# A ring of nine gathered rows, with weight loads of one 512 KB tile instead of two at a time

## The chip, the cores and the metric

The kernel runs on one core of one Trainium2 chip. The metric is device time in microseconds (us) of one execution, lower is better. Before the change three runs gave a median of 2445.37 us (2445.34 to 2450.84).

## The reference, cut to what matters

A block of 512 tokens by 1024 channels, all in fp32. Per token, after two mixers, come a product with an output matrix, a product with a query matrix, and the PEER layer: the queries are scored against two sets of 128 keys, the 16 best pairs for each of 8 heads name 128 experts out of 16384, and for each of them the layer computes

```python
dot = h @ u[expert]                # u and v rows of 1024 numbers
y  += gate * gelu(dot) * v[expert]
```

The kernel keeps u and v side by side (`peer_uv`), so one expert is one row of 8 KB. Then a second block follows: an input product of six 512-column tiles (`w_in_2`), two kinds of attention, an output product (`w_out_2`), and a gated feed-forward layer with 2816 hidden channels (`w_gu`, `w_down_2`).

## The kernel before, in words

Tokens are worked on in four blocks of 128. The program has a front part (to about 329 us), then `stage_first` (to about 1982 us), which runs the PEER layer for all four blocks and beside it the second block's work for the first 256 tokens, and `stage_half`, the second block's work for the last 256 tokens, alone.

**Gather** (class `Gather`). A slot is one (block, expert place): 512 slots. For slot n GpSimd issues an indirect DMA (L1123) that fetches one row of 8 KB for each of the 128 tokens, 1 MB in all, into buffer n mod RING of `uv_ring`. RING is the eighth argument at L2539, 8 before. VectorE takes the dot product with the u half (L1275), ScalarE the gelu, the weight (L1325) and a diagonal matrix of the weights (L1334), and TensorE multiplies it with the v half in four passes (L1355). In the last block each fourth slot is added by VectorE instead (L1229). Gather n waits until slot n - RING has been added (`added`).

**Weights** (class `Weights`, L1391 to L1450). All other products of these two stages take their weights as tiles of 256 by 512 numbers, 512 KB. A tile goes through three steps: SyncE loads it into a raw buffer (`loads`, L1413), ScalarE rounds it to a high part (`highs`, L1427), VectorE or GpSimd subtracts that from the raw tile for the low part (`lows`, L1435), and TensorE makes twelve matmuls of it (`product`, L1446 to L1448). Before the change a load carries a pair of tiles, 1 MB, and there are two raw buffers of a pair. Load m, of tiles 2m and 2m+1, waits until the low part of tile 2m-3 is done:

```python
if m >= self.RAW:
    sp.wait_ge(self.s_lo, 2 * (m - self.RAW + 1))
```

There are `SPLIT` buffers for high and low parts, two in `stage_first` and three in `stage_half`; `highs` waits until TensorE has used tile n - SPLIT. `stage_first` takes 146 tiles: `Tail` a (24, partly before the gather), `Tail` b (24), `In2` (24), `Out2` (8), `Ffn` (66). `stage_half` takes 98.

**Order of work.** Each engine's program is one list, merged by `weave` from several streams by planned places in us. The plan gives a slot 2.6 us and a tile 2.8 us (`Tail` a), 9.0 us (`Tail` b) or 4.2 us (`In2`, `Out2`, `Ffn` of the first half). Each engine then runs its list in order, so what waits holds back all that stands behind it on that engine. Loads are placed 20 us ahead of their tile; gather n is placed at the slot time of n - RING + 2.5.

Of the kernel before, what the change touches and what calls it, by code (L numbers as in the profile page):

```python
# [19 lines left out]
P = 128  # L20
S = 512
D = 1024
KD = D // P
TB = S // P
# [37 lines left out]
class Chain:  # L62
# [3 lines left out]
    def __init__(self, eng, sem):  # L66
        self.eng, self.sem, self.n, self.base = eng, sem, 0, 0
# [103 lines left out]
class Columns:  # L171
# [11 lines left out]
    def loads(self, sp):  # L183
        for n in range(len(self.src)):
            self.load(sp, n)
# [830 lines left out]
class Gather:  # L1016
# [189 lines left out]
    def dve(self, dve):  # L1206
# [55 lines left out]
        for place, _, b, s in queue:  # L1262
# [33 lines left out]
        for q in range(self.n - G, self.n):  # L1296
            if self.here(q):
                add(q)
# [87 lines left out]
class Weights:  # L1386
# [4 lines left out]
    def __init__(self, K, ctx, raw, split, us):  # L1391
        self.K, self.us, self.src, self.at = K, us, [], []
        self.RAW, self.SPLIT, self.LEAD = raw, split, split - 1
        self.raw = [K.sb(ctx, f"w_raw{r}", [P, 2 * self.KK, 512]) for r in range(self.RAW)]
        self.hi = [K.sb(ctx, f"w_high{r}", [P, self.KK, 512], F32R) for r in range(self.SPLIT)]
        self.lo = [K.sb(ctx, f"w_low{r}", [P, self.KK, 512], F32R) for r in range(self.SPLIT)]
        self.s_land = [K.sem(f"weights_landed{r}") for r in range(self.RAW)]
        self.s_hi, self.s_lo, self.s_used = K.sem("weights_high"), K.sem("weights_low"), K.sem("weights_used")

    def add(self, pairs, places):  # L1400

        first = len(self.at)
        assert len(places) == 2 * len(pairs)
        self.src += pairs
        self.at += places
        return first

    def loads(self, sp):
        for m, src in enumerate(self.src):
            yield self.at[2 * m] - 20.0  # L1410
            if m >= self.RAW:
                sp.wait_ge(self.s_lo, 2 * (m - self.RAW + 1))
            sp.dma_start(self.raw[m % self.RAW][:, :, :], src).then_inc(self.s_land[m % self.RAW], 16)  # L1413

    def tile(self, n):
        return self.raw[n // 2 % self.RAW][:, self.KK * (n % 2):self.KK * (n % 2 + 1), :]

    def place(self, n):
        return max(self.at[n - self.LEAD], self.at[n] - 15.0) if n >= self.LEAD else self.at[0] - 5.0

    def highs(self, act):
        for n in range(len(self.at)):
            yield self.place(n)
            act.wait_ge(self.s_land[n // 2 % self.RAW], 16 * (n // 2 // self.RAW + 1))
            if n >= self.SPLIT:
                act.wait_ge(self.s_used, n - self.SPLIT + 1)
            act.copy(self.hi[n % self.SPLIT][:, :, :], self.tile(n)).then_inc(self.s_hi, 1)  # L1427

    def lows(self, eng, first=0, last=None):
        for n in range(first, len(self.at) if last is None else last):  # L1430
            yield self.place(n)
            if n == first and n:
                eng.wait_ge(self.s_lo, n)
            eng.wait_ge(self.s_hi, n + 1)
            eng.tensor_tensor(self.lo[n % self.SPLIT][:, :, :], self.tile(n),  # L1435
                               self.hi[n % self.SPLIT][:, :, :].bitcast(F32), ALU.subtract).then_inc(self.s_lo, 1)

    def product(self, pe, n, rows, banks, k0, first, last):
# [143 lines left out]
class In2:  # L1582
# [4 lines left out]
    def __init__(self, K, W, plan, half, h, nat, one=False):  # L1587
        self.K, self.W, self.h, self.half, self.nat, self.one = K, W, h, half, nat, one
        self.nb = half.nb
        self.CH = KD // W.KK  # L1590
        self.at = plan.take([W.us] * (6 * self.CH) + [half.tail_us])
        self.first = W.add([K.i["w_in_2"][self.TILE[t], c] for t in self.ORDER for c in range(self.CH // 2)],
                           self.at[:6 * self.CH])
# [464 lines left out]
class Out2:  # L2058


    def __init__(self, K, W, plan, half, mix, banks):
        self.K, self.W, self.half, self.mix, self.banks, self.nb = K, W, half, mix, banks, half.nb
        self.CH = KD // W.KK
        self.at = plan.take([W.us] * (2 * self.CH))
        self.first = W.add([K.i["w_out_2"][n, c] for n in range(2) for c in range(self.CH // 2)], self.at[:2 * self.CH])
        self.s_x = K.sem("out2_added")

    def pe(self, pe):
# [18 lines left out]
class Ffn:  # L2087
# [4 lines left out]
    def __init__(self, K, W, plan, half, h, up, acc):  # L2092
        self.K, self.W, self.half, self.h, self.up, self.acc, self.nb = K, W, half, h, up, acc, half.nb
        self.CH = KD // W.KK
        lengths, tiles, self.order = [], [], []
        for g in range(self.G + 1):
            if g < self.G:
                for c in range(self.CH):
                    self.order.append(("up", g, c))
                tiles += [K.i["w_gu"][g, c] for c in range(self.CH // 2)]  # L2100
            if g:
                self.order.append(("down", g - 1, 0))
                tiles.append(K.i["w_down_2"][g - 1])
            if g < self.G:
                self.order.append(("turn", g, 0))
            if g:
                self.order.append(("down", g - 1, 1))
        self.lag = half.lag
# [112 lines left out]
class Tail:  # L2221
# [4 lines left out]
    def __init__(self, K, W, plan, b0, x, split, keep, us, gap, before=None, prompt=0):  # L2226
# [5 lines left out]
        self.first_o = W.add([K.i["w_out_1"][n, c] for n in range(2) for c in range(self.CH // 2)], self.at_o[:2 * self.CH])  # L2232
# [7 lines left out]
        self.first = W.add([K.i["w_peer_q"][j, c] for j in range(self.G) for c in range(self.CH // 2)],  # L2240
                           self.at_p[:self.G * self.CH])
        self.end = self.at_p[-1]
        self.at_t = [self.rowed(j) + 1.0 if j < prompt else self.at_p[self.CH * (j + 1) + 2] for j in range(self.G - 1)]
# [290 lines left out]
def stage_first(K, half, x):  # L2534

    nc, nb = K.nc, half.nb
    with ExitStack() as c1:
        half.place(c1, x[0:nb], False)
        g = Gather(K, c1, list(range(TB)), x, 0.0, 2.6, (6, 7), 8, 4, 3)  # L2539
        W, plan, un = Weights(K, c1, 2, 2, half.tile_us), Plan(), half.mix  # L2540
        begin = g.at(nb * SLOTS + 4)
        four = [K.ps[j][:, :] for j in range(4)]
# [129 lines left out]
def stage_half(K, half, x):  # L2672

    nc, nb = K.nc, half.nb
    with ExitStack() as ctx:
        half.place(ctx, x, True)
        half.place_queries(ctx)
        W, plan = Weights(K, ctx, 2, 3, half.tile_us), Plan()
        un = half.spare.rearrange("p (b d) -> p b d", b=nb)
        four = [K.ps[j][:, :] for j in range(4)]  # L2680
        at = plan.take([half.tail_us])
# [127 lines left out]
def _pairs(_np, w):  # L2809

    r, c = w.shape
    return w.reshape(r // 512, 4, 128, c // 512, 512).transpose(3, 0, 2, 1, 4)


def _columns(_np, w):

    return w.reshape(KD, P, -1, P).transpose(2, 1, 0, 3).reshape(-1, P, D)
# [37 lines left out]
```

## Time and profile before

| | |
|---|---|
| median of three runs | 2445.37 us |
| the profiled execution's own time | 2446.69 us |
| its span (first to last instruction) | 2445.0 us |
| TensorE busy | 2046.7 us (84%) |
| VectorE busy | 1501.4 us (61%) |
| ScalarE busy | 995.8 us (41%) |
| GpSimd busy | 920.9 us (38%) |
| bytes moved by DMA | 726.58 MB, 540.59 of them on the gather's queue |
| 1 MB weight loads in all | 122: 73 in the first stage, 49 in the second |

Busy shares are means over stages with different limits. The DMA line of the page, in 40 slices of 61 us, shows which stages keep the 16 DMA engines full. A `_a` at the end of a name is `stage_first`, `_b` is `stage_half`. GB/s divided by the share of the DMA engines in a window tells at what rate they work while they are busy.

### The profile page before, as it was taken

How to read it: one execution, taken by the hardware profiler on the slowest of the kernel's cores; microseconds unless marked ns; L12 is line 12 of the kernel's file. 1: busy time of each engine (PE TensorE's matmuls, PEld its weight loads, DVE VectorE, ACT ScalarE, POOL GpSimd, SP SyncE). 2: the span in 40 equal slices, each digit the busy share in tenths (PEclk: the TensorE clock that was granted, in tenths of full speed). 3: DMA queues.
4: the chain of work that ended last, by engine and by line, in shares of the span. 5: the costliest groups of instructions: out<-in, count | busy, mean ns of one | idle time of the engine just before them, and what ended most of it. 6: DMA issues, size and time to landing. Idle time of an engine off the chain costs nothing. (4 is left out here: it accounts for less than half of the span.)

```text
span 2445.0 us, 22099 instructions
## 1 busy us (share of the span) xinstructions
PE 2046.7 (84%) x7187; PEld 1273.7 (52%) x7187; DVE 1501.4 (61%) x2987; ACT 995.8 (41%) x2304; POOL 920.9 (38%) x681
## 2 busy tenths in 40 slices
PE   7997867897898777777899888879999968687999
PEld 4776645553554222222465334446666547456787
DVE  4748546788895677755678876667777732442111
ACT  3205443434233222232545577444344334344443
POOL 3522002333444433333223444233343326005887
PEclk8986678999999999999899999889999989798999
DMA  7720035999999999999899999999999934002554
GB/s 266 271 93 1 1 137 204 378 421 378 421 394 391 418 421 422 421 421 421 340 384 388 417 372 369 376 369 383 421 421 421 421 142 145 18 1 99 177 190 155
DMA packets 111071, 726.58 MB, mean 297 GB/s; under 512 B 12520, under 2 KB 13547, under 8 KB 29803
## 3 DMA queue, kind: packets, MB, share of 16 engines
q0 software_dynamic: 74800, 540.59, 54.2%
q1 hardware_dynamic: 35520, 184.43, 20.2%
q8 instruction: 57, 0.93, 0.2%
q14 instruction: 60, 0.48, 0.1%
q10 hardware_dynamic: 634, 0.14, 0.0%
HBM read 716.45 MB, written 8.66 MB: 297 GB/s over the span
## 5 line engine op out<-in xcount | busy, mean ns | idle before, releaser
L1355 PE MATMUL ps<-uv_ring_a,expert_diag_a 128*128 128x512 f32 x1920 | 906.8, 617 | 213.8 <-ACT expert_diag_a L1334 195.0
L1123 POOL DMA_INDIRECT uv_ring_a<-in_peer_uv_dram,expert_idx x512 | 582.2, 1137 | 958.1 <-PE ps L1355 918.3
L1275 DVE CUSTOM_DVE_ANT_0 uv_ring_a<-uv_ring_a,x_rows 128x1024 f32<-128x1024 f32 x512 | 620.4, 1219 | 170.8 <-DMA uv_ring_a<-in_peer_uv_dram,expert_idx 170.0
L1355 PEld LDWEIGHTS ps<-uv_ring_a,expert_diag_a 128*128 128x128 f32 x1920 | 364.0, 196 | 674.6 <-issue 362.2
L1319 ACT ACTIVATE expert_gelu_a<-expert_dot_a 128x2 f32<-128x2 f32 x256 | 52.1, 204 | 782.9 <-DVE expert_dot_a L1275 782.7
L1435 POOL TENSOR_TENSOR w_low_b<-w_raw_b,w_high_b 128x1024 fp32r<-128x1024 f32 x98 | 233.7, 2395 | 256.5 <-ACT w_high_b L1427 255.5
L1435 DVE TENSOR_TENSOR w_low_a<-w_raw_a,w_high_a 128x1024 fp32r<-128x1024 f32 x142 | 173.6, 1223 | 192.2 <-ACT w_high_a L1427 191.5
L1427 ACT CAST w_high_a<-w_raw_a 128x1024 fp32r<-128x1024 f32 x146 | 151.0, 1038 | 97.3 <-PE ps L1448 85.4
L1334 ACT ACTIVATE expert_diag_a<-ident,expert_weight_a 128x128 f32<-128x128 f32 x480 | 168.6, 395 | 0.6 <-ACT expert_weight_a L1325 0.6
L1427 ACT CAST w_high_b<-w_raw_b 128x1024 fp32r<-128x1024 f32 x98 | 102.7, 1052 | 122.3 <-PE ps L1448 68.2
L1325 ACT ACTIVATE expert_weight_a<-expert_gelu_a,expert_gate 128x1 f32<-128x1 f32 x512 | 122.8, 286 | 8.9
L1446 PE MATMUL ps<-w_high_a,turned_high_a 128*128 128x512 f32 x208 | 101.3, 487 | 5.8 <-DVE ffn_low_a L2200 5.7
L1446 PE MATMUL ps<-w_high_a,tail_turned_high_a 128*128 128x512 f32 x192 | 89.0, 463 | 17.6 <-DVE w_low_a L1435 11.7
L2190 DVE SCALAR_TENSOR_TENSOR ffn_silu_b<-ffn_silu_b,ps 128x256 f32<-128x256 f32 x22 | 9.2, 417 | 142.2 <-ACT ffn_silu_b L2172 142.2
L1446 PE MATMUL ps<-w_high_b,turned_high_b 128*128 128x512 f32 x208 | 82.6, 397 | 3.9 <-DVE turned_low_b L1484 3.9
L1448 PE MATMUL ps<-w_high_a,turned_low_a 128*128 128x512 f32 x208 | 83.4, 401 | 0.0
L1447 PE MATMUL ps<-w_low_a,turned_high_a 128*128 128x512 f32 x208 | 83.0, 399 | 0.0
L1447 PE MATMUL ps<-w_low_b,turned_high_b 128*128 128x512 f32 x208 | 82.3, 396 | 0.0
L1448 PE MATMUL ps<-w_high_b,turned_low_b 128*128 128x512 f32 x208 | 82.1, 395 | 0.0
L1447 PE MATMUL ps<-w_low_a,tail_turned_high_a 128*128 128x512 f32 x192 | 77.7, 405 | 0.0
L1448 PE MATMUL ps<-w_high_a,tail_turned_low_a 128*128 128x512 f32 x192 | 77.4, 403 | 0.0
L203 POOL TENSOR_TENSOR in_low<-in_raw,in_high 128x1024 fp32r<-128x1024 f32 x20 | 54.4, 2725 | 55.3 <-ACT in_high L198 55.2
(460 smaller groups left out, 3279.1 us busy)
## 6 DMA issues: line engine op xcount, KB each, us to landing
w_raw_a<-in_w_gu_dram SPq DMA_DIRECT2D x22, 1024.0 KB, 9.0
w_raw_b<-in_w_gu_dram SPq DMA_DIRECT2D x22, 1024.0 KB, 4.9
w_raw_a<-in_w_peer_q_dram SPq DMA_DIRECT2D x16, 1024.0 KB, 9.2
w_raw_a<-in_w_out_dram SPq DMA_DIRECT2D x12, 1024.0 KB, 9.0
w_raw_a<-in_w_in_dram SPq DMA_DIRECT2D x12, 1024.0 KB, 9.8
w_raw_b<-in_w_in_dram SPq DMA_DIRECT2D x12, 1024.0 KB, 4.9
w_raw_a<-in_w_down_dram SPq DMA_DIRECT2D x11, 1024.0 KB, 9.1
w_raw_b<-in_w_down_dram SPq DMA_DIRECT2D x11, 1024.0 KB, 4.9
```

Of the source, the lines that this page charges most:

```text
L203: pool.tensor_tensor(self.lo[n % self.SPLIT][:, :], self.raw[n % self.RAW][:, :], self.hi[n % self.SPLIT][:, :].bitcast(F32), ALU.subtract ...
L1123: pool.indirect_dma_start(out=self.ring[:, n % self.RING, :], out_offset=None, in_=K.uv, in_offset=bass.IndirectOffsetOnAxis(ap=K.idx[self ...
L1275: dve.tensor_tensor_reduce(u, u, self.h[b][:, :], 1.0, 0.0, ALU.mult, ALU.add, self.a[:, s:s + 1]).then_inc(self.s_dot, 1)
L1319: act.activation(self.gl[:, c], self.a[:, c], ACT.Gelu).then_inc(self.s_gelu, 1)
L1325: act.activation(self.w[:, i:i + 1], self.gl[:, i:i + 1], ACT.Copy, scale=K.gate[self.blocks[b] % 2][:, i:i + 1]).then_inc(self.s_w, 1)
L1334: act.activation(self.diag[q % self.DIAGS][:, :], K.ident[:, :], ACT.Copy, scale=self.w[:, i:i + 1]).then_inc(self.s_diag, 1)
L1355: ins = nc.tensor.matmul(self.bank(half), self.diag[q % self.DIAGS][:, :], self.ring[:, n % self.RING, D + 512 * half:D + 512 * half + 512 ...
L1427: act.copy(self.hi[n % self.SPLIT][:, :, :], self.tile(n)).then_inc(self.s_hi, 1)
L1435: eng.tensor_tensor(self.lo[n % self.SPLIT][:, :, :], self.tile(n), self.hi[n % self.SPLIT][:, :, :].bitcast(F32), ALU.subtract).then_inc( ...
L1446: nc.tensor.matmul(bank, rh, hi[:, kk, :], start=first and kk == 0, stop=False)
L1447: nc.tensor.matmul(bank, rh, lo[:, kk, :], start=False, stop=False)
L1448: ins = nc.tensor.matmul(bank, rl, hi[:, kk, :], start=False, stop=last and kk == self.KK - 1)
```

## The change

The ring gets a ninth buffer (8 KB per partition). The raw weight buffers hold one tile in place of two: in `stage_first` two of 512 KB in place of two of 1 MB, in `stage_half` four of 512 KB in place of two of 1 MB. Each load carries one tile; load n waits for the low part of tile n - 2 (first stage) or n - 4 (second). The weights are laid out in DRAM tile by tile, so a partition's piece of a load is 4 KB in place of 8 KB. No instruction of ScalarE, VectorE, GpSimd or TensorE is added or removed; SyncE issues 244 weight loads in place of 122.

```diff
-        self.raw = [K.sb(ctx, f"w_raw{r}", [P, 2 * self.KK, 512]) for r in range(self.RAW)]
+        self.raw = [K.sb(ctx, f"w_raw{r}", [P, self.KK, 512]) for r in range(self.RAW)]
...
     def loads(self, sp):
-        for m, src in enumerate(self.src):
-            yield self.at[2 * m] - 20.0
-            if m >= self.RAW:
-                sp.wait_ge(self.s_lo, 2 * (m - self.RAW + 1))
-            sp.dma_start(self.raw[m % self.RAW][:, :, :], src).then_inc(self.s_land[m % self.RAW], 16)
+        for n, src in enumerate(self.src):
+            yield self.at[n] - 20.0
+            if n >= self.RAW:
+                sp.wait_ge(self.s_lo, n - self.RAW + 1)
+            sp.dma_start(self.raw[n % self.RAW][:, :, :], src).then_inc(self.s_land[n % self.RAW], 16)
...
     def highs(self, act):
-        for n in range(len(self.at)):
+        for n in range(len(self.src)):
             yield self.place(n)
-            act.wait_ge(self.s_land[n // 2 % self.RAW], 16 * (n // 2 // self.RAW + 1))
+            act.wait_ge(self.s_land[n % self.RAW], 16 * (n // self.RAW + 1))
...
-        g = Gather(K, c1, list(range(TB)), x, 0.0, 2.6, (6, 7), 8, 4, 3)
+        g = Gather(K, c1, list(range(TB)), x, 0.0, 2.6, (6, 7), 9, 4, 3)
         W, plan, un = Weights(K, c1, 2, 2, half.tile_us), Plan(), half.mix
...
-        W, plan = Weights(K, ctx, 2, 3, half.tile_us), Plan()
+        W, plan = Weights(K, ctx, 4, 3, half.tile_us), Plan()
...
-    inputs["w_peer_q"] = _pairs(_np, inputs["w_peer_q"][0])
-    for name in ("w_in_2", "w_out_2"):
-        inputs[name] = _pairs(_np, inputs[name][0])
+    inputs["w_peer_q"] = _tiles(_np, inputs["w_peer_q"][0])
+    for name in ("w_in_2", "w_out_2", "w_down_2"):
+        inputs[name] = _tiles(_np, inputs[name][0])
```

The other edits of the diff let `Tail`, `In2`, `Out2` and `Ffn` name single tiles in place of pairs to `Weights.add`. `_pairs` laid out four rows of 128 by 512 per load, `_tiles` lays out two.

## Rows read from the trace of the kernel before

**Rows 1.** The page: the DMA engines' busy tenths in 40 slices.
```profile
DMA  7720035999999999999899999999999934002554
```

**Rows 2.** Windows: us, busy per engine (instructions), clock, DMA share, GB/s.
```profile
750.00:1150.00 400.00, 293.93 (x668) 119.73 (x667) 252.96 (x582) 106.88 (x397) 159.17 (x156) 0.98 1.01 417
...
1550.00:1700.00 150.00, 129.22 (x415) 79.68 (x416) 100.90 (x150) 66.83 (x152) 49.86 (x43) 0.92 0.90 366
1700.00:1950.00 250.00, 238.84 (x827) 153.82 (x826) 188.28 (x272) 99.00 (x255) 96.84 (x78) 0.99 1.01 421
```

**Rows 3.** Waits in 413 to 1968 us: total us, times, longest.
```profile
POOL uv_ring_a L1123 <- PE ps L1355: 918.3, 418, 16.3
...
DVE uv_ring_a L1275 <- DMA uv_ring_a<-in_peer_uv_dram,expert_idx: 170.0, 162, 3.3
```

**Rows 4.** Windows of the large dips of the DMA share, columns as in rows 2.
```profile
440.00:451.00 11.00, 11.00 (x50) 7.95 (x49) 8.85 (x23) 4.70 (x14) 3.04 (x3) 1.00 0.71 264
586.00:594.00 8.00, 8.00 (x13) 3.48 (x14) 6.32 (x25) 6.33 (x15) 2.71 (x2) 0.68 0.43 148
...
1170.00:1178.00 8.00, 6.72 (x22) 3.69 (x23) 3.78 (x16) 2.12 (x8) 1.87 (x2) 0.70 0.43 150
1181.00:1188.00 7.00, 6.84 (x15) 3.53 (x16) 6.61 (x17) 2.69 (x8) 2.62 (x2) 0.76 0.44 146
...
1549.00:1558.00 9.00, 6.36 (x9) 2.77 (x10) 8.51 (x13) 1.93 (x5) 0.94 (x1) 0.62 0.37 127
...
1618.00:1626.00 8.00, 7.25 (x18) 4.05 (x19) 5.97 (x9) 2.91 (x9) 2.37 (x2) 0.79 0.41 146
1652.00:1658.00 6.00, 6.00 (x19) 3.60 (x18) 3.43 (x4) 2.33 (x2) 2.11 (x2) 0.95 0.47 160
```

**Rows 5.** GpSimd's timeline at the dip of 586 to 594 us.
```profile
590.04 1.77 POOL L1123 DMA_INDIRECT uv_ring_a<-in_peer_uv_dram,expert_idx  x1 [9.20 <-PE ps L1355]
```

**Rows 6.** DMA in 1700 to 1900 us: queue, packets, MB, share; a load's median us.
```profile
q1 hardware_dynamic: 2769, 20.19, 24.3%
...
w_raw_a<-in_w_gu_dram SPq DMA_DIRECT2D x13, 1024.0 KB, 9.0
```

**Rows 7.** DMA in 926 to 937 us, then a load in 1535 to 1546.
```profile
q1 hardware_dynamic: 144, 0.52, 11.8%
...
route_scores_a<-s_dram SPq DMA_DIRECT2D x1, 512.0 KB, 8.0
...
x_rows<-x_rows_dram SPq DMA_DIRECT2D x1, 512.0 KB, 8.4
```

**Rows 8.** DMA in 1960 to 1970 us, after the last gather; then in 2250 to 2440.
```profile
x_rows<-x_rows_dram SPq DMA_DIRECT2D x1, 512.0 KB, 3.5
...
w_raw_b<-in_w_gu_dram SPq DMA_DIRECT2D x19, 1024.0 KB, 4.9
```

**Rows 9.** Timelines of VectorE and ScalarE before the gather starts.
```profile
343.90 1.23 DVE L1435 TENSOR_TENSOR w_low_a<-w_raw_a,w_high_a 128x1024 fp32r<-128x1024 f32 x1 [5.07 <-ACT w_high_a L1427]
...
348.32 1.05 ACT L1427 CAST w_high_a<-w_raw_a 128x1024 fp32r<-128x1024 f32 x1 [1.71 <-PE ps L1448]
```

**Rows 10.** The same two timelines just after the gather has started.
```profile
413.28 1.22 DVE L1435 TENSOR_TENSOR w_low_a<-w_raw_a,w_high_a 128x1024 fp32r<-128x1024 f32 x1
...
417.74 1.05 ACT L1427 CAST w_high_a<-w_raw_a 128x1024 fp32r<-128x1024 f32 x1 [1.42 <-PE ps L1448]
```

**Rows 11.** The tile's instructions in 1700 to 1950 us, and one tile's steps there.
```profile
L1435 DVE TENSOR_TENSOR w_low_a<-w_raw_a,w_high_a x48: 1210/1225/1227, 1699.6 to 1947.9; 128x1024 fp32r<-128x1024 f32 x48
...
1753.77 1.23 DVE L1435 TENSOR_TENSOR w_low_a<-w_raw_a,w_high_a 128x1024 fp32r<-128x1024 f32 x1 [2.33 <-ACT w_high_a L1427]
...
1760.78 1.05 ACT L1427 CAST w_high_a<-w_raw_a 128x1024 fp32r<-128x1024 f32 x1 [1.50 <-PE ps L1448]
...
1762.80 1.22 DVE L1435 TENSOR_TENSOR w_low_a<-w_raw_a,w_high_a 128x1024 fp32r<-128x1024 f32 x1
```

**Rows 12.** TensorE's timeline at the start of the second stage.
```profile
1999.79 0.76 PE L1446 MATMUL ps<-w_high_b,in_turned_high_b 128*128 128x512 f32 x1 [8.21 <-POOL w_low_b L1435]
```

More of the change, by code:

```diff
@@ L1398, in __init__, with add @@
         self.s_hi, self.s_lo, self.s_used = K.sem("weights_high"), K.sem("weights_low"), K.sem("weights_used")
[L1400 to L1404, printed above, removed]
+    def add(self, tiles, places):
+        first = len(self.src)
+        self.src += tiles
         self.at += places
@@ L1408, in loads @@
     def loads(self, sp):
-        for m, src in enumerate(self.src):
-            yield self.at[2 * m] - 20.0
-            if m >= self.RAW:
-                sp.wait_ge(self.s_lo, 2 * (m - self.RAW + 1))
-            sp.dma_start(self.raw[m % self.RAW][:, :, :], src).then_inc(self.s_land[m % self.RAW], 16)
-    def tile(self, n):
-        return self.raw[n // 2 % self.RAW][:, self.KK * (n % 2):self.KK * (n % 2 + 1), :]
+        for n, src in enumerate(self.src):
[3 more added lines that the diff above has]
+            sp.dma_start(self.raw[n % self.RAW][:, :, :], src).then_inc(self.s_land[n % self.RAW], 16)
     def place(self, n):
@@ L1421, in highs @@
     def highs(self, act):
-        for n in range(len(self.at)):
+        for n in range(len(self.src)):
             yield self.place(n)
-            act.wait_ge(self.s_land[n // 2 % self.RAW], 16 * (n // 2 // self.RAW + 1))
+            act.wait_ge(self.s_land[n % self.RAW], 16 * (n // self.RAW + 1))
             if n >= self.SPLIT:
                 act.wait_ge(self.s_used, n - self.SPLIT + 1)
-            act.copy(self.hi[n % self.SPLIT][:, :, :], self.tile(n)).then_inc(self.s_hi, 1)
+            act.copy(self.hi[n % self.SPLIT][:, :, :], self.raw[n % self.RAW][:, :, :]).then_inc(self.s_hi, 1)
     def lows(self, eng, first=0, last=None):
-        for n in range(first, len(self.at) if last is None else last):
+        for n in range(first, len(self.src) if last is None else last):
             yield self.place(n)
@@ L1434, in lows @@
             eng.wait_ge(self.s_hi, n + 1)
-            eng.tensor_tensor(self.lo[n % self.SPLIT][:, :, :], self.tile(n),
+            eng.tensor_tensor(self.lo[n % self.SPLIT][:, :, :], self.raw[n % self.RAW][:, :, :],
                                self.hi[n % self.SPLIT][:, :, :].bitcast(F32), ALU.subtract).then_inc(self.s_lo, 1)
@@ L1591, in __init__ @@
         self.at = plan.take([W.us] * (6 * self.CH) + [half.tail_us])
-        self.first = W.add([K.i["w_in_2"][self.TILE[t], c] for t in self.ORDER for c in range(self.CH // 2)],
+        self.first = W.add([K.i["w_in_2"][self.TILE[t], c] for t in self.ORDER for c in range(self.CH)],
                            self.at[:6 * self.CH])
@@ L2064, in __init__ @@
         self.at = plan.take([W.us] * (2 * self.CH))
-        self.first = W.add([K.i["w_out_2"][n, c] for n in range(2) for c in range(self.CH // 2)], self.at[:2 * self.CH])
+        self.first = W.add([K.i["w_out_2"][n, c] for n in range(2) for c in range(self.CH)], self.at[:2 * self.CH])
         self.s_x = K.sem("out2_added")
@@ L2099, in __init__ @@
                     self.order.append(("up", g, c))
-                tiles += [K.i["w_gu"][g, c] for c in range(self.CH // 2)]
+                    tiles.append(K.i["w_gu"][g, c])
             if g:
                 self.order.append(("down", g - 1, 0))
-                tiles.append(K.i["w_down_2"][g - 1])
+                tiles.append(K.i["w_down_2"][0, g - 1])
             if g < self.G:
@@ L2107, in __init__ @@
                 self.order.append(("down", g - 1, 1))
+                tiles.append(K.i["w_down_2"][1, g - 1])
         self.lag = half.lag
@@ L2231, in __init__ @@
         self.at_o = plan.take([us] * (2 * self.CH))
-        self.first_o = W.add([K.i["w_out_1"][n, c] for n in range(2) for c in range(self.CH // 2)], self.at_o[:2 * self.CH])
+        self.first_o = W.add([K.i["w_out_1"][n, c] for n in range(2) for c in range(self.CH)], self.at_o[:2 * self.CH])
         self.at_n = plan.take([gap, gap])
@@ L2239, in __init__ @@
         self.at_p += plan.take([us / 2] * 4)
-        self.first = W.add([K.i["w_peer_q"][j, c] for j in range(self.G) for c in range(self.CH // 2)],
+        self.first = W.add([K.i["w_peer_q"][j, c] for j in range(self.G) for c in range(self.CH)],
                            self.at_p[:self.G * self.CH])
@@ L2806, in _tiles @@
     return w.reshape(r // 256, 2, 128, c // 512, 512).transpose(3, 0, 2, 1, 4)
-def _pairs(_np, w):
-    r, c = w.shape
-    return w.reshape(r // 512, 4, 128, c // 512, 512).transpose(3, 0, 2, 1, 4)
 def _columns(_np, w):
@@ L2829 @@
     gate, up = inputs.pop("w_gate_2")[0], inputs.pop("w_up_2")[0]
-    inputs["w_gu"] = _pairs(_np, _np.concatenate([gate.reshape(D, -1, 256), up.reshape(D, -1, 256)], axis=2).reshape(D, -1))
+    inputs["w_gu"] = _tiles(_np, _np.concatenate([gate.reshape(D, -1, 256), up.reshape(D, -1, 256)], axis=2).reshape(D, -1))
     inputs["c_columns"] = inputs.pop("c")[0].reshape(KD, P).T
@@ L2841 @@
     wo = inputs.pop("w_out")[0]
-    inputs["w_out_1"] = _pairs(_np, _np.concatenate([wo[0:512], wo[512:][heads]]))
-    inputs["w_peer_q"] = _pairs(_np, inputs["w_peer_q"][0])
-    for name in ("w_in_2", "w_out_2"):
-        inputs[name] = _pairs(_np, inputs[name][0])
-    inputs["w_down_2"] = inputs["w_down_2"][0].reshape(-1, 2, 128, 2, 512).transpose(0, 2, 3, 1, 4).reshape(-1, 128, 4, 512)
+    inputs["w_out_1"] = _tiles(_np, _np.concatenate([wo[0:512], wo[512:][heads]]))
+    inputs["w_peer_q"] = _tiles(_np, inputs["w_peer_q"][0])
+    for name in ("w_in_2", "w_out_2", "w_down_2"):
+        inputs[name] = _tiles(_np, inputs[name][0])
     for name in _INS:
```

## The prediction

> **What bounds the kernel now.** I read the DMA line of the page first [rows 1]: nine tenths from slice 8 to slice 32, some 1500 of 2445 us. That is the gather. The windows say how full it is [rows 2]: from 750 to 1150 us and from 1700 to 1950 us the share is 1.01, at 417 and 421 GB/s, so nothing is left there; from 1550 to 1700 us it is 0.90. A gather moves 1.05 MB, at 421 GB/s 2.5 us. In the stretch 1700 to 1950 TensorE is also busy 238.84 of 250 us: two bounds lie within 5% of each other, and in that stretch the feed-forward tiles of the first half run between the slots.
>
> The waits say the same from the other side [rows 3]. GpSimd waits 918.3 us in 418 waits for TensorE to free a ring buffer, and VectorE 170.0 us for gathered rows. A ring that is always full is no loss while the DMA engines are full. It is one where they run dry. So I looked for the dips of the share. The large ones are short windows of their own [rows 4]. Idle time is length times (1 - share): 3.2 us at 440 to 451; then 4.6, 4.6, 3.9, 5.7, 4.7 and 3.2 us, 26.6 us in the six from 586 on. In the first of these GpSimd stood still 9.20 us until TensorE released a buffer [rows 5]: TensorE, held up by something else, freed no buffer, and the eight rows on their way ran out.
>
> **The ring of nine.** Gather n is released by slot n - 9. In each dip one more gather, 2.5 us of DMA work, is under way before the engines run dry, and as the stretch behind it is again full, the 2.5 us stay won. Every one of the six dips is longer than that. The four up to 1558 us give 4 x 2.5 = 10 us. The two behind lie where TensorE is nearly full too, and I count half, 2.5 us. So -12.5 us. Ends: 0 (TensorE's hold-up grows by what the ring adds), and -26.6 us, all that was idle there.
>
> The dip at 440 is dealt with below. The ring adds no instruction; GpSimd issues the same 512 gathers, each placed 2.6 us earlier, and the only other work on its list in that stage, four low parts and the loads before the gather, is planned ahead of the first gather either way.
>
> **Single tiles: what a load takes.** Beside the gather a 1 MB load lands 9.0 us after issue [rows 6]. For 512 KB with 4 KB per partition there are loads of just this shape, of scores and of token rows: 8.0 and 8.4 us [rows 7]. Half the bytes save one microsecond, no more, since each packet still stands in line behind a gathered row's. Without the gather it is 3.5 us against 4.9 us for 1 MB [rows 8]. I take 8.0 and 3.5.
>
> A weight load may start when the low part of tile n - 2 is done; before, of tile 2m - 3, so three to four tiles ahead. The loop of one buffer is load, high, low: with the gather 8.0 + 0.05 to issue + 1.05 + 1.22 + 0.1 for two handovers = 10.4 us, for two tiles.
>
> **Before the gather.** Tile 4's high part starts at 348.32, 3.2 us after the low part of tile 2 ended (343.90 + 1.23) [rows 9]. The load needs 3.5. So 0.3 us is lost where tiles follow closely. There are two such runs before the gather, of six and eight tiles, and the loss shows in every second tile at most: 1 us of the path, since the routing that starts the gather waits for these products. Ends 0 and 4 (a 512 KB load beside other loads, 4.9 in place of 3.5, in three places).
>
> **The gather's start.** Now the first eight gathers fill the DMA queues while the last six tiles of `Tail` a are still to come. The high part at 417.74 stands 3.2 us after the low part that ended at 414.50 [rows 10]; the load takes 8.0, so it is 4.8 us late, and its successors lose a little more. TensorE does the first slots between these tiles, so the ring opens late, and the dip at 440 to 451 grows by about that; the ninth buffer gives 2.5 us back. I take +4. Ends 0 and 8.
>
> **`Tail` b, `In2`, `Out2`.** `Tail` b is planned at 9.0 us a tile, 18 for two, against a loop of 10.4: hidden. `In2` and `Out2` are 32 tiles in which DMA or TensorE sets a pace somewhat above that of the feed-forward part, and I count nothing; if that cover is gone, they are part of the second rival. On SyncE a load that waits holds back stores and loads of rows and scores behind it. Each has its loads spaced a tile apart now, so the wait of one is shorter, and I count nothing.
>
> **The feed-forward tiles of the first half.** 48 low parts from 1699.6 to 1947.9 [rows 11] are (1947.9 - 1699.6) / 47 = 5.28 us a tile, 10.57 us for two. The loop is 10.4. It fits with 0.17 us to spare, if nothing comes between. Something does: the tile shown [rows 11] had its high part at 1760.78, done at 1761.83, and its low part at 1762.80, 0.97 us later, since VectorE was at something else. By its load it would be later still: 1755.00 + 0.05 + 8.0 = 1763.05, 2.3 us behind 1760.78. Most tiles are done some microseconds before TensorE wants them, and that lead takes up single delays, but not a loop that is too long in the mean. I take half of the 0.97 as the mean delay in a loop: 10.4 + 0.49 - 10.57 = 0.3 us for two tiles, 33 times, 10 us, and of these 8 kept, as TensorE's idle 4.5% takes up some. Behind a late load ScalarE holds the diagonals too, which is in the same 8. Ends 0 and 27: with a load of 9.0, as the 1 MB one has, the loop is 11.4, which is 0.83 too long for two tiles, 33 times.
>
> **Twice the packets.** A half MB cost 11.8% of 11 us, 1.30 us, as 4 KB pieces [rows 7], and 24.3% of 200 us for 20.19 MB, 1.26 us, as 8 KB pieces [rows 6]. 0.04 us for each of 128 tiles beside the gather is 5 us if the DMA engines were the bound throughout; I take 3, ends 0 and 5. SyncE's 122 additional issues are hidden, it is idle nearly always.
>
> The Trainium skill ("DMA: Bandwidth & Descriptors", Rules for kernel authors) asks for 1 MiB or more per DMA for the best bandwidth, which speaks against this change. Its fit there, 2.0 us plus bytes / 436e3, gives an estimate of 3.2 us for 512 KB and 4.4 for 1 MB; without the gather the rows agree nearly (3.5, 4.9), with it they don't (8.0, 9.0), and by that fit the 8 us of the feed-forward part and the 4 at the gather's start would be none, and the sum 12 us lower.
>
> **The second stage.** TensorE waits 8.21 us for the first tile's low part, until 1999.79 [rows 12]. The first load is 1 MB, and half of it would land 0.5 MB / 421 = 1.2 us sooner: -1.2 us. With four tiles in flight and 3.5 us a load the later loads are early by several microseconds instead of just in time, but TensorE hardly waits for them now. Ends 0 and -3.
>
> **Sum.** -12.5 + 1 + 4 + 8 + 3 - 1.2 = +2.3 us on the profiled execution's 2446.7 us, so 2449.0. That execution is 1.3 us above the median of the runs, and against the median I say 2448. What this kernel's measurement can tell from no change is about 0.3%, 7.3 us: the forecast is no change (chance 0.38).
>
> **Rivals.**
> *Weights become the bound (slower, 0.37).* Place: feed-forward tiles between slots, 1600 to 1970 us, and the 24 tiles of `In2`. It decides as soon as the loop of load, high and low takes over 10.6 us. For it: 10.4 from rows without any delay in it. Against it: when TensorE stalls, fewer gathers are released and a load then waits less. Price at 9.0 us per load or a like delay: 27 + 8 at the start + 1 + 3, less the ring's 10 before that stretch and 1.2: +28, which is 2474.
> *The ring's gain comes whole and the loads stay hidden (faster, 0.25).* -26.6 + 1 + 4 + 3 - 1.2 = -20: 2426. With 15 (2.5 in each of six dips) it would be -8: 2437. For it: the dips are there, and each began with a full ring. Against it: TensorE's hold-ups aren't shortened by a ring, only bridged.
> *The ring does nothing* since the DMA engines are full, and the loads cost what I say: +15, 2461, inside the slower case.
> *The change doesn't do what it says:* the raw buffers and the ring have the same bytes before and after, and gather n has a buffer of its own, so I give that nothing.
>
> The range that leaves out no more than 2 in 10 is 2431 to 2477; the forecast's own is 2440 to 2453. Faster by over 0.3%: 0.25. Within: 0.38. Slower: 0.37.
>
> **What would show it.** In the profile after: a 512 KB weight load at 8.0 to 8.4 us beside the gather and about 3.5 in the second stage; the dips at about 590, 1170, 1185 and 1550 us shorter by 2.5 us each; waits of ScalarE at L1427 for the landing of raw tiles, of which there are hardly any in the gather now, and waits of TensorE for low parts; more than 5.3 us a tile after 1700 us; TensorE's first tile of the second stage 1.2 us sooner behind its transposes. Wrong would be: loads of 6 us or less beside the gather (then the faster case), or dips that are as long as before (then the ring gave nothing), or 1.01 of share in the feed-forward part with a span as before though loads are late.

## The result, and the profile after

The kernel after the change takes 2472.35 us (median of 4 runs, 2467.99 to 2475.6), against 2445.36 before. The ratio is 1.0107, with a 95% interval of 1.0084 to 1.0131: 26 us slower, and the range of that is 21 to 32. The forecast was 2448, no change; the time is within 2 us of the first rival's (2474). The profiled execution has a span of 2473.2 us, 28.2 above before.

The page's DMA line, to be laid beside [rows 1]. It hardly tells that anything was lost: only slices 8 and 27 fell from nine to eight, and in the feed-forward stretch, slices 28 to 32, all are still nines. (A slice is 61.8 us now, 61.1 before.)

```profile
DMA  7720045899999999999899999989999945003664
```

Two windows as in [rows 2]. In 250 us of the feed-forward stretch TensorE now does 768 matmuls in place of 827, VectorE 250 instructions in place of 272, and the DMA engines move 395 GB/s in place of 421. That is 6% less, while their busy share went from 1.01 to 0.99, 2% less: the share alone would not have told it. TensorE, VectorE and ScalarE all do less in the same time, and none of the three is full: something that they all wait for sets the pace. It isn't TensorE's clock, granted at 0.97 in place of 0.99 here: over the first stage the same 208 product matmuls took 487 ns each before and 488 after (L1446 and L1441 on the pages).

```profile
1550.00:1700.00 150.00, 120.33 (x381) 74.02 (x382) 96.56 (x146) 63.82 (x148) 47.54 (x40) 0.91 0.91 363
1700.00:1950.00 250.00, 227.40 (x768) 143.79 (x767) 173.97 (x250) 92.79 (x235) 90.33 (x73) 0.97 0.99 395
```

The loads, from the page's list of DMA issues (KB each, median us to landing). Half the bytes take 7.9 us beside the gather, where 1 MB took 9.0 [rows 6], and 3.6 us in the second stage, where it took 4.9 [rows 8].

```profile
w_raw_a<-in_w_gu_dram SPq DMA_DIRECT2D x44, 512.0 KB, 7.9
w_raw_b<-in_w_gu_dram SPq DMA_DIRECT2D x44, 512.0 KB, 3.6
```

Then the waits in 413 to 2000 us (engine, line, waited for: total us, times, longest). ScalarE stands and waits for a weight load in 37 places, 106 us in all. Before, the same list had one such row, 4.0 us, shown last. A wait isn't yet a cost: the longest, 13.7 us at a `w_out` tile at 489 us, stands as 12.8 us in the kernel r8_four too, which is level with before.

```profile
ACT w_high_a L1422 <- DMA w_raw_a<-in_w_down_dram: 28.7, 13, 4.6
ACT w_high_a L1422 <- DMA w_raw_a<-in_w_gu_dram: 23.3, 9, 4.0
ACT w_high_a L1422 <- DMA w_raw_a<-in_w_peer_q_dram: 23.3, 7, 5.6
ACT w_high_a L1422 <- DMA w_raw_a<-in_w_out_dram: 17.1, 3, 13.7
PE ps L1441 <- DVE w_low_a L1430: 13.7, 7, 3.2
ACT w_high_a L1422 <- DMA w_raw_a<-in_w_in_dram: 13.6, 5, 6.3
...
ACT w_high_a L1427 <- DMA w_raw_a<-in_w_out_dram: 4.0, 1, 4.0
```

The pace of the tiles, to set beside [rows 11], and the landing times of that stretch (min, median, max): (1945.4 - 1700.8) / 43 = 5.69 us a tile in place of 5.28. The four lines between say how long an engine stood idle before the instructions of this stretch, and how often: VectorE until ScalarE's cast was done, 42 times in 44 subtractions; ScalarE until the load landed, 11 and 7 times in 45 casts, or until TensorE was done with a buffer, 2 times.

```profile
L1430 DVE TENSOR_TENSOR w_low_a<-w_raw_a,w_high_a x44: 1219/1225/1228, 1700.8 to 1945.4; 128x1024 fp32r<-128x1024 f32 x44
...
  ACT w_high_a L1422: 76.0, 42
  DMA w_raw_a<-in_w_down_dram: 25.3, 11
  DMA w_raw_a<-in_w_gu_dram: 15.9, 7
  PE ps L1443: 4.8, 2
...
DMA to landing us min/median/max: 4.3/7.8/9.6
```

At the gather's start ScalarE's timeline shows the six last tiles of `Tail` a, each of them now released by its load. The last cast is at 446.52, 35.1 us after the first gather (411.4). Before, it was at 437.38 (last line), 24.2 us after the first gather (413.2).

```profile
420.11 1.04 ACT L1422 CAST w_high_a<-w_raw_a 128x1024 fp32r<-128x1024 f32 x1 [5.20 <-DMA w_raw_a<-in_w_peer_q_dram]
...
446.52 1.05 ACT L1422 CAST w_high_a<-w_raw_a 128x1024 fp32r<-128x1024 f32 x1 [3.61 <-DMA w_raw_a<-in_w_peer_q_dram]
...
437.38 1.05 ACT L1427 CAST w_high_a<-w_raw_a 128x1024 fp32r<-128x1024 f32 x1 [1.43 <-PE ps L1448]
```

Before the gather little is lost. SyncE's timelines begin the stage with its first weight loads, after and then before: 85.9 us (411.4 - 325.5) and 84.1 us (413.2 - 329.1) ahead of the first gather.

```profile
325.49 24.72 SPq L1411 DMA_DIRECT2D w_raw_a<-in_w_out_dram  x7
...
329.10 19.13 SPq L1413 DMA_DIRECT2D w_raw_a<-in_w_out_dram  x4
```

The dips of [rows 4], found again in the trace of after. Idle time is 4.6, 2.6, 3.8, 1.4, 4.5 and 4.3 us, in place of 4.6, 4.6, 3.9, 5.7, 4.7 and 3.2: 21.2 in place of 26.6. Two are shorter, the one at 1174 us by 2.0 and the one at the change to the last block by 4.3; the other four are about as long as before, or longer.

```profile
594.00:604.00 10.00, 8.73 (x15) 3.87 (x16) 8.05 (x28) 7.61 (x19) 3.44 (x3) 0.70 0.54 197
1174.00:1181.00 7.00, 6.71 (x24) 3.68 (x24) 2.98 (x12) 1.60 (x6) 1.87 (x2) 0.80 0.63 222
1184.00:1192.00 8.00, 8.00 (x22) 4.39 (x21) 6.92 (x21) 3.38 (x11) 2.53 (x2) 0.81 0.53 190
1558.00:1563.00 5.00, 5.00 (x13) 2.35 (x12) 4.79 (x7) 2.50 (x9) 2.71 (x2) 0.89 0.72 259
1623.00:1632.00 9.00, 8.21 (x21) 4.66 (x22) 6.67 (x10) 2.95 (x9) 3.21 (x2) 0.81 0.50 178
1655.00:1664.00 9.00, 9.00 (x27) 5.92 (x26) 4.09 (x6) 3.92 (x5) 2.81 (x2) 0.83 0.52 181
```

And TensorE's first tile of the second stage waits 7.06 us for its low part, in place of 8.21 [rows 12].

```profile
2028.75 0.76 PE L1441 MATMUL ps<-w_high_b,in_turned_high_b 128*128 128x512 f32 x1 [7.06 <-POOL w_low_b L1430]
```

Where the 28 us of the profiled execution went is told by three points in time: the first gather, the end of the third of the four blocks of 128 tokens (L1247, where VectorE adds a block's sum), and the last gather. The first gather is at 411.4 us after and at 413.2 before. From there the third block ends 1140.9 and 1135.4 us later, and the last gather is issued 1559.8 and 1531.6 us later. So the kernel after is 5 us behind when the last block begins, and loses 23 us in the last block, where the feed-forward tiles run between the slots. The lines are after and then before.

```profile
1552.35 0.69 DVE L1247 TENSOR_TENSOR expert_sum_a<-ps,gate_rows 128x512 f32<-128x512 f32 x1 [0.59 <-DMA x_rows<-x_rows_dram]
L1123 POOL DMA_INDIRECT uv_ring_a<-in_peer_uv_dram,expert_idx x512: 932/940/2222, 411.4 to 1971.2; - x171
...
1548.59 0.68 DVE L1247 TENSOR_TENSOR expert_sum_a<-ps,gate_rows 128x512 f32<-128x512 f32 x1
L1123 POOL DMA_INDIRECT uv_ring_a<-in_peer_uv_dram,expert_idx x512: 932/940/1997, 413.2 to 1944.8; - x171
```

### The profile page after: what moved, and what is told of

The parts are those of the page before. It is cut to its first block and busy times, and to the rows that moved or that the text cites. A ratio compares the mean times of both kernels' runs of the same rounds, so it can differ in the third digit from the quotient of the medians.

```text
span 2473.2 us, 22221 instructions
## 1 busy us (share of the span) xinstructions
PE 2059.6 (83%) x7187; PEld 1276.6 (52%) x7187; DVE 1499.3 (61%) x2987; ACT 996.9 (40%) x2304; POOL 926.2 (37%) x681
## 5 line engine op out<-in xcount | busy, mean ns | idle before, releaser
L1355 PE MATMUL ps<-uv_ring_a,expert_diag_a 128*128 128x512 f32 x1920 | 921.1, 626 | 217.7 <-ACT expert_diag_a L1334 198.3
L1355 PEld LDWEIGHTS ps<-uv_ring_a,expert_diag_a 128*128 128x128 f32 x1920 | 370.0, 199 | 687.4 <-issue 373.0
L1441 PE MATMUL ps<-w_high_a,tail_turned_high_a 128*128 128x512 f32 x192 | 88.8, 463 | 23.6 <-DVE w_low_a L1430 18.8
L1441 PE MATMUL ps<-w_high_a,turned_high_a 128*128 128x512 f32 x208 | 101.4, 488 | 7.6 <-DVE ffn_low_a L2196 7.5
L1441 PE MATMUL ps<-w_high_b,turned_high_b 128*128 128x512 f32 x208 | 82.6, 397 | 3.9 <-DVE turned_low_b L1479 3.9
```

The source lines that it names most:

```text
L1355: ins = nc.tensor.matmul(self.bank(half), self.diag[q % self.DIAGS][:, :], self.ring[:, n % self.RING, D + 512 * half:D + 512 * half + 512 ...
L1441: nc.tensor.matmul(bank, rh, hi[:, kk, :], start=first and kk == 0, stop=False)
```

## The experiments

Times are given as ratios to the kernel before, measured beside each kernel on the same chip, with a 95% interval. From chip to chip the median of before moved from 2443 to 2447 us, so the ratios are what is to be compared. Where two ratios are subtracted below, the difference is uncertain by 6 to 12 us. A stretch of one trace seems steadier than a whole time (r8_four and r9_both, each traced twice, took 1532.9 and 1532.1 us, and 1525.8 and 1527.3 us, from the first gather to the last), but it is one execution.

### More buffers, and the ring back to eight

**r8_two** is the kernel after with the ring of before:

```diff
-        g = Gather(K, c1, list(range(TB)), x, 0.0, 2.6, (6, 7), 9, 4, 3)
+        g = Gather(K, c1, list(range(TB)), x, 0.0, 2.6, (6, 7), 8, 4, 3)
```

> The kernel after the change with the ring put back to eight; the raw buffers stay two single tiles. Theory A (the loop of load, high part and low part over two single buffers sets the pace of the feed-forward tiles, and the ninth ring buffer wins back a part): the feed-forward part loses at least as much as after the change, a tile takes 5.6 us or more from 1700 us on, and the ring's part is missing on top: 2474 to 2490 us. Theory B (the ninth buffer does the harm: more gathered rows stand in line ahead of a weight load): the load lands sooner and the time falls back to 2445 to 2455. Theory C (smaller packets cost DMA time): within 3 us of the kernel after, 2469 to 2476.

Measured: 2484.54 us, 1.0159 (1.0121 to 1.0197). Theory A; B falls. Without the ninth buffer the single tiles cost 39 us, with it 26.

**r8_three** and **r8_four** have the ring of eight and three or four single raw buffers in the first stage (the diff is that of three; the other has a 4 there):

```diff
-        W, plan, un = Weights(K, c1, 2, 2, half.tile_us), Plan(), half.mix
+        W, plan, un = Weights(K, c1, 3, 2, half.tile_us), Plan(), half.mix
```

> Ring of eight, three single raw buffers in the first stage in place of two. Theory A: the loop of 10.4 us now covers three tiles (15.8 us), no tile is late, and ScalarE hardly waits for raw tiles after 450 us: 2443 to 2450 us, with 5.3 us a tile from 1700 us on. Theory B: the same, so it doesn't speak on B. Theory C (packets of 4 KB cost DMA time by themselves): still 10 us or more above before, 2455 to 2475.

> Ring of eight, four single raw buffers in the first stage: the bytes of before, only in four single tiles in place of two pairs. Theory A: as with three, 2443 to 2449 us, since three already hide the loop. Theory C: 2455 to 2475, as packets and loads are as small as after the change. If four are clearly faster than three (over 5 us), a loop of three buffers was still late somewhere, most likely where the gather starts.

Measured: three 2445.1 us, 1.0011 (0.9987 to 1.0035); four 2441.2 us, 0.9991 (0.9968 to 1.0014), and when measured again 0.9983 (0.9965 to 1.0001). One more buffer of 512 KB brings back 36 us of the 39 (1.0159 - 1.0011), and the kernel is then level with before within its interval. Four are not clearly faster than three; 2441.2 lies 2 us below the range expected for it. The tiles of r8_three in 1700 to 1950 us:

```profile
L1430 DVE TENSOR_TENSOR w_low_a<-w_raw_a,w_high_a x48: 1214/1224/1227, 1699.2 to 1947.8; 128x1024 fp32r<-128x1024 f32 x48
```

(1947.8 - 1699.2) / 47 = 5.29 us a tile, that of before. ScalarE waits for a raw tile five times after the first gather and never after 476 us. All loads of r8_four are as small and as many as after the change, and it is level with before: Theory C falls. What the smaller pieces cost in DMA rate shows in the windows: in 1700 to 1950 us r8_three, r8_four, r9_late4 and r9_both all move 418 GB/s, where before moves 421.

### The packets alone

**pairs_4k** is the kernel before, one load for two tiles, with the two tiles laid out apart in DRAM:

```diff
-            sp.dma_start(self.raw[m % self.RAW][:, :, :], src).then_inc(self.s_land[m % self.RAW], 16)
+            sp.dma_start(self.raw[m % self.RAW][:, :, :].rearrange("p (t k) c -> p t k c", t=2),
+                         src.rearrange("t p k c -> p t k c")).then_inc(self.s_land[m % self.RAW], 16)
```

> The kernel before (ring of eight, two pairs of 1 MB, one load for a pair), with the weights laid out as after the change, so that a partition's part of a load is two pieces of 4 KB in place of one of 8 KB. Theory A with my reading of why half a load takes nearly as long (each weight packet stands in line behind one gathered row's packet): a 1 MB load takes 11 to 13 us beside the gather in place of 9.0; the pair's loop has room for that in the feed-forward part (about 15 us between release and need), so 2445 to 2455 us. If a load's time goes by its bytes and not by its packets: 9 us as before and 2445. Theory C: 2455 or more.

Measured: 2455.14 us, 1.0040 (1.0020 to 1.0060), 10 us slower, where r8_four with the same packets isn't. That is the border between what Theory A and Theory C had been given (2455), so this run alone doesn't decide between them; r8_four does. Its trace tells no landing times for these loads beside the gather, so the 11 to 13 us expected for one stay untested; in the second stage a pair lands in 5.0 us, where it was 4.9. What the trace shows are waits of ScalarE for raw tiles, nine in all and 26.4 us, where before had one of 4.0 us (columns as above; a ninth is 1.2 us). The 8.3 us are at the gather's start, at 424 us.

```profile
ACT w_high_a L1428 <- DMA w_raw_a<-in_w_down_dram: 10.9, 6, 3.5
ACT w_high_a L1428 <- DMA w_raw_a<-in_w_peer_q_dram: 8.3, 1, 8.3
ACT w_high_a L1428 <- DMA w_raw_a<-in_w_out_dram: 6.0, 1, 6.0
...
L1123 POOL DMA_INDIRECT uv_ring_a<-in_peer_uv_dram,expert_idx x512: 932/938/2121, 407.1 to 1947.2; - x171
```

So a pair in 4 KB pieces lands later than one in 8 KB pieces, late enough to be waited for. That fits the reading that a packet stands in line behind a gathered row's packet whatever its own size; it isn't shown by a landing time. From the first gather to the last it takes 1540.1 us, where before takes 1531.6: 8.5 of the 10 us lie in that stretch.

### What a ring buffer is worth

**before_r7** is the kernel before with a ring of seven (the argument 8 at L2539 made 7).

> The kernel before with a ring of seven, loads of pairs as they are: what one ring buffer is worth while no weight is late. Theory D (each dip of the DMA share is bridged 2.5 us per buffer, in six large dips and some small ones): 12 to 25 us slower than before, 2455 to 2468. Theory E (a buffer only helps where late weights hold TensorE up, as in the pair of kernels with two single buffers): within 4 us of before, 2439 to 2447.

Measured: 2469.92 us, 1.0100 (1.0073 to 1.0127), 24 us slower, at the upper end of what Theory D gave. Theory E is out: a buffer is worth something where no weight is late. The first and the last gather issue in its trace (the kernel's start differs by several microseconds from run to run, so the difference of the two is to be read; the line of before stands above the experiments):

```profile
L1123 POOL DMA_INDIRECT uv_ring_a<-in_peer_uv_dram,expert_idx x512: 932/938/2010, 402.0 to 1961.5; - x171
```

1559.5 us against 1531.6. The DMA engines' share over the gather, windows of before and then before_r7:

```profile
413.00:1960.00 1547.00, 1307.06 (x3885) 707.33 (x3885) 1121.06 (x2333) 633.03 (x1689) 582.20 (x512) 0.96 0.98 399
```

```profile
402.00:1973.00 1571.00, 1320.21 (x3886) 710.49 (x3886) 1123.77 (x2332) 632.93 (x1689) 580.71 (x512) 0.96 0.97 393
```

### Buffers lent by memory that is free at the time

A third raw buffer beside a ring of nine would take 4 KB per partition more than the kernels before and after have; no run tried whether it fits. But two places of 8 KB per partition are idle just where tiles are late: the ninth ring buffer until gather 8, and the two route-score buffers once the last experts are chosen. **r9_late4** is the kernel after with four buffers from tile 80 on, **r9_early4** with four for tiles 0 to 23, **r9_both** has both. Tiles 0 to 23 lie in part before the gather, and gather 8 has to wait for the loan to end. `spans` says which buffers a range of tiles goes round; loads and casts look their buffer up there.

```diff
+            W.spans = [(0, 24, [0, 1, 2, 3]), (24, 48, [0, 1]), (48, 80, [0, 1]), (80, 1 << 30, [0, 1])]
+            W.raw += [g.ring[:, g.RING - 1, D * i:D * i + D].rearrange("p (k c) -> p k c", k=2) for i in range(2)]
+            W.s_land += [K.sem(f"weights_landed_in_ring{i}") for i in range(2)]
+            g.first_free = (W.s_lo, 24)
...
+        W.raw += [g.sw[i][:, :, :].rearrange("p a b -> p (a b)").rearrange("p (k c) -> p k c", k=2) for i in range(2)]
+        W.s_land += [K.sem(f"weights_landed_in_scores{i}") for i in range(2)]
+        W.spans[-1] = (80, 1 << 30, [0, 1, late, late + 1])
+        W.before[82] = [(g.s_idx, len(g.groups))]
```

> The kernel after the change (ring of nine, two single raw buffers), but from tile 80 on, the feed-forward part of the first half, two more single buffers: the tiles lie in the two route-score buffers, free once the last experts are chosen. Theory A: the 25 us that slots and tiles lose against before between tiles 82 and 145 go, the rest stays: 2443 to 2451 us, 5.3 us a tile from 1700 us on. If something else in the feed-forward part made it slow (more packets, the ring ahead of the loads), under 10 us come back: 2460 to 2472.

> The kernel after the change with four single raw buffers for the first 24 tiles alone (before and at the start of the gather): the two more lie in the ninth ring buffer, which gather 8 then takes over when the low part of tile 23 is done. Theory A: the tiles at the gather's start are no longer late, 4 to 8 us come back: 2463 to 2470 us. If the stretch behind, which is full of DMA, had made good for it anyway: within 3 us of the kernel after, 2469 to 2475.

> Both of it: ring of nine, four single raw buffers for tiles 0 to 23 and from tile 80 on, two between. Theory A with D (a ring buffer is worth 10 us or more by itself): 2430 to 2441 us, below both kernels. Theory A with E (worth nothing while no weight is late): 2440 to 2447, level with before. Over 2450: theory A is wrong on where the loss comes from.

Measured, the three beside before on one chip, the kernel after by itself (its row is that of the result):

| | us | ratio to before | interval |
|---|---|---|---|
| after | 2472.35 | 1.0107 | 1.0084 to 1.0131 |
| r9_late4 | 2450.44 | 1.0011 | 0.9991 to 1.0030 |
| r9_early4 | 2462.12 | 1.0056 | 1.0035 to 1.0077 |
| r9_both | 2437.41 | 0.9955 | 0.9936 to 0.9975 |

Four buffers for the feed-forward tiles give back 0.0096, 24 us; four at the start 0.0051, 12 us (4 to 8 had been expected); both 0.0152, 37 us, about the sum of the two. The first two are uncertain by 8 us each. The windows of the feed-forward stretch, r9_late4, are those of before again but for the GB/s (418, where 421 was):

```profile
1700.00:1950.00 250.00, 239.89 (x838) 154.84 (x837) 187.43 (x273) 99.78 (x255) 97.93 (x79) 0.99 1.02 418
```

The 12 us of the start are two parts. In r9_early4 the first gather comes 81.1 us after the first weight load (410.8 - 329.7), where after had 85.9, and the gathers take 1551.9 us, where after had 1559.8: 4.8 and 7.9 us. In r9_both the last tile of `Tail` a is cast 24.4 us after the first gather (411.3), from the ninth ring buffer; after had it at 35.1, before at 24.2:

```profile
435.73 1.05 ACT L1439 CAST w_high_a<-uv_ring_a 128x1024 fp32r<-128x1024 f32 x1 [4.28 <-DMA uv_ring_a<-in_w_peer_q_dram]
...
329.69 0.91 SPq L1428 DMA_DIRECT2D w_raw_a<-in_w_out_dram  x2
L1125 POOL DMA_INDIRECT uv_ring_a<-in_peer_uv_dram,expert_idx x512: 932/938/2262, 410.8 to 1962.7; - x171
```

(The first line is of r9_both, the last two are of r9_early4.)

### The ninth buffer where no feed-forward tile is late, and the repeat

> The kernel r9_late4 with a ring of eight: two single buffers up to tile 79, four from tile 80 on. Against r8_two it tells what the feed-forward tiles lose without the ninth buffer, against r9_late4 what the ninth buffer is worth where no feed-forward tile is late. Theory A with D (a ring buffer is worth 10 us or more by itself): 1.0055 to 1.009 of before, 11 to 16 us above r9_late4. If the ninth buffer only helped against late tiles: within 4 us of r9_late4, about 1.001 to 1.003.

> The kernel r9_both once more, beside r8_four on the same chip, to have the gain of the ninth buffer against the same bytes used as four single tiles. If the earlier difference of the two (0.9955 and 0.9991 of before) holds: 8 to 10 us below r8_four, 9 to 13 us below before.

> The kernel r8_four once more, for the comparison on one chip: 0.997 to 1.001 of before.

r8_late4 is r9_late4 with the 9 made 8; the other two are r9_both and r8_four once more. Measured: r8_late4 2462.7 us, 1.0075 (1.0046 to 1.0104); r9_both 2435.97 us, 0.9952 (0.9934 to 0.9969); r8_four 2442.95 us, 0.9983 (0.9965 to 1.0001). All three are as expected. So the ninth buffer is worth 16 us between r8_late4 and r9_late4 (uncertain by 9) and 13 us between r8_two and the kernel after (by 11): no difference is seen between late feed-forward tiles and none. The first and last gather issue say it more sharply. For r8_late4 and then r9_late4 they are 1550.8 and 1535.8 us apart, 15 us; for r8_two (414.8 to 1989.3) and the kernel after 1574.5 and 1559.8, again 15:

```profile
L1123 POOL DMA_INDIRECT uv_ring_a<-in_peer_uv_dram,expert_idx x512: 932/939/2426, 410.3 to 1961.1; - x171
```

```profile
L1123 POOL DMA_INDIRECT uv_ring_a<-in_peer_uv_dram,expert_idx x512: 932/938/1989, 413.7 to 1949.5; - x171
```

The ends of the blocks, in r8_late4 and then r9_late4, say where these 15 us are won. From the first gather the first block ends 420.4 and 411.6 us later, the third 1151.3 and 1140.5. So 9 of the 15 us come in the first block, 2 in the second and third together, and 4 in the last.

```profile
830.71 0.69 DVE L1247 TENSOR_TENSOR expert_sum_a<-ps,gate_rows 128x512 f32<-128x512 f32 x1 [2.52 <-DMA x_rows<-x_rows_dram]
1561.65 0.69 DVE L1247 TENSOR_TENSOR expert_sum_a<-ps,gate_rows 128x512 f32<-128x512 f32 x1 [1.02 <-DMA x_rows<-x_rows_dram]
...
825.28 0.69 DVE L1247 TENSOR_TENSOR expert_sum_a<-ps,gate_rows 128x512 f32<-128x512 f32 x1 [2.82 <-DMA x_rows<-x_rows_dram]
1554.22 0.69 DVE L1247 TENSOR_TENSOR expert_sum_a<-ps,gate_rows 128x512 f32<-128x512 f32 x1 [0.79 <-DMA x_rows<-x_rows_dram]
```

r9_both, with the bytes of SBUF that the kernels before and after have, was faster than before both times, by 11 and 12 us, and below r8_four, measured beside it, by 0.003, 8 us.

## Why the prediction was right, and where it was wrong

The range held the time, and the rival that it named, weights that become the bound, is what happened. The forecast itself, no change at 2448, was wrong. That the rival's price of 2474 lies within 2 us of the time is partly luck: it took a load of 9.0 us "or a like delay" in the feed-forward part, and what came was a load of 7.8 us and a delay of another kind. Term by term:

- **The ring, -12.5.** Measured 13 and 16 us, in two pairs of kernels that differ in the ring alone, and 15 us in the traces of both pairs. The size was right, the places were not, and so the size was partly luck. The forecast had 2.5 us in each of four large dips up to 1558 us and half as much in two more. Measured, 9 of 15 us come in the first block, which has one of the six dips, and 2 in the next two blocks, which have two. At the start of the last block, behind the fourth dip, the two traces are still no more than 10.8 us apart (L1226, at 1568.1 in r8_late4 and 1560.7 in r9_late4). What the gain consists of isn't shown; the smaller dips, which the forecast left out, are a candidate that no run took apart. Nor is a ring buffer worth the same everywhere: from eight to seven costs 24 us, and from r8_four to r9_both, where the start isn't late and the ninth buffer is lent out at first, it brings 8.
- **The loads, 8.0 and 3.5.** Measured 7.8 in the stretch (7.7 to 8.0 over the kinds of weights) and 3.6. These came from loads of the same shape and company elsewhere in the trace, and they hold.
- **The feed-forward tiles, +8.** This is the term that was mis-sized. Measured 24 us (r9_late4 against after), and 0.0084, 21 us, with a ring of eight (r8_late4 against r8_two). The loop was right in kind: two tiles take 11.38 us, of which 7.8 are the load, 1.04 the cast, 1.23 the subtraction and 0.1 hand-overs. The remainder is 1.2 us, where I had 0.49. Its place was wrong too. I had taken it from a tile whose subtraction waited for VectorE. After the change VectorE stood idle and waited for the cast before 42 of 44 subtractions, so it can hardly have held a tile up; and ScalarE waited for a load before 18 of 45 casts. In the others the landed tile stood until ScalarE came to it: there the remainder lies, because ScalarE has other work in the order of its list, or the tile's high buffer was still in use (2 times). With the pace that was measured, 33 x (11.38 - 10.57) = 27 us, against 24 from the runs. I had also let TensorE's idle 4.5% take up some. It took up next to nothing; that all engines and the gather are tied to one order there would explain it, but no run shows that by itself.
- **The gather's start, +4 (0 to 8).** The gathers take 7.9 us less with four buffers there (r9_early4 against after), and the last cast, 24.2 us after the first gather before, went to 35.1, 10.9 us later: at my upper end or above it. I worked out the first late tile (4.8 us, and it came 5.2 us late) and let the others lose a little more; but all six waited for their load, 22.6 us in all. The ring had been meant to give 2.5 us back there. No run shows that by itself.
- **Before the gather, +1 (0 to 4).** 85.9 us in place of 84.1 from the first weight load to the first gather, +1.8. With four buffers it is 81.1, so the two single ones cost 4.8 us there against four: the other part of the 12 us of r9_early4.
- **Packets, +3.** r8_four carries the same packets and twice the loads and is at 0.9991 and 0.9983, so they cost little if the loads are far enough ahead. In the stretch of the feed-forward tiles they take 418 GB/s in place of 421; estimated from that, 0.7% of 250 us is 1.8 us for 48 tiles, 0.04 us a tile, which is what I had worked out. pairs_4k, at 1.0040, says that they cost more where a load's landing is waited for.
- **`In2`, `Out2`, nothing.** ScalarE waited 13.6 us for `w_in` loads there, so the loop of two did bind for moments. No run takes that alone away; r9_both still has such waits (14.9 us), and is 11 us below before.
- **The second stage, -1.2.** TensorE's wait for its first tile went from 8.21 to 7.06: -1.15. No run takes the second stage alone.

The runs add up without any term of the forecast: r9_both is 11 us below before, and to take its four buffers away at the two places costs 24 and 12 us: +25, where the ratio says 26 (21 to 32). The likeliest case was picked badly for a reason that the text had in it: a loop of 10.4 us in a pace of 10.57 leaves 0.17 us for three in-order engines, and the row beside it already showed 0.97 gone in one loop. (That row's 0.97 was in front of VectorE, and the delay that came was in front of ScalarE; as a warning it was right.) That is no margin, and the case in which the loop binds should have been the forecast.

The rule of the Trainium skill for 1 MiB and more per DMA ("DMA: Bandwidth & Descriptors", Rules for kernel authors) spoke against the change, and the time went its way; but r8_four, all in 512 KB loads, is level with before, so in this kernel it isn't bandwidth that small loads cost. It is how many of them are in flight: with two at 1.0159, with three at 1.0011. The fit that the forecast took from the same page (Anatomy of one DMA) is given there for DMAs issued from GpSimd. SyncE's loads of 512 KB took 3.6 us without the gather, where it gives an estimate of 3.2, and 7.9 beside it.

## What to carry to other kernels

A buffer's round trip is its load under the traffic that is really there, plus each step that must come before its next load, plus what each in-order engine makes it wait; here that last part was 1.2 us of 11.4, where 0.4 (10.57 - 10.17) was to spare, and decided the matter. Halving a load beside this gather saved about one microsecond of nine (9.0 and 7.9). So a buffer of half the bytes comes round in nearly the time of a whole one, and brings half: count buffers in round trips, not in bytes. Three such buffers, 1.5 MB in place of 2, were enough. And before taking memory from a buffer, look for memory that is idle in the stretch where it is short: two loans of 8 KB turned the same trade from 26 us lost into 11 us won.

## What the runs showed of the hardware that I had not expected

A ring buffer is worth 13 to 24 us in the pairs that differ in it alone, although the DMA engines' share over the whole gather is 0.98 before and 0.97 with one less. One hundredth of 1550 us is 15.5 us, so a share rounded like this hides what is at stake. The busy share also falls less than the bytes moved: in the stretch of the late feed-forward tiles it was 0.99 where it had been 1.01, with 395 GB/s in place of 421. Engines that show as nearly always busy moved 6% less. So read the bytes per second beside the share.

And the same 4 KB pieces cost 10 us in 1 MB loads (pairs_4k) and nothing that could be measured in 512 KB loads four deep (r8_four).
